# Input and forget gates of an mLSTM from the unnormalised input: split products on the normalised input against one full-precision product in four column groups

## The reference, cut to what matters

```python
def rms_norm(x, g):
    xf = x.astype(jnp.float32)
    out = xf * lax.rsqrt(jnp.mean(xf * xf, axis=-1, keepdims=True) + EPS)
    return (out * g.astype(jnp.float32)).astype(x.dtype)
...
    xn = rms_norm(x, lp['norm1_g'])
    z = xn @ lp['w_in'] + lp['b_in']
    sizes = [D_LRU, D_ML, D_ML, D_ML, D_ML, ML_HEADS, ML_HEADS, D_MODEL]
    u, q, k, v, o, ipre, fpre, ga, gb = jnp.split(z, np.cumsum(sizes).tolist(), axis=-1)
```

## Time and profile before

| what | value |
|---|---|
| time, median of 3 runs | 1068.19 us (1068.11 to 1069.31) |
| the profiled execution's own time | 1067.82 us |
| its span in the profile | 1066.0 us |
| TensorE (PE) busy | 1054.0 us, 99% |
| VectorE (DVE) busy | 620.0 us, 58% |
| ScalarE (ACT) busy | 388.5 us, 36% |
| GpSimd (POOL) busy | 371.1 us, 35% |
| granted clock of TensorE, mean | 0.999 |

### The profile page before, as it was taken

One profiled execution on the slowest core, in us unless ns is written; L12 is line 12 of the kernel. 1 busy time (PEld: TensorE's weight loads), 2 busy tenths in 40 slices (PEclk: granted clock), 3 DMA queues, 4 the chain that ended last, 5 costly groups with the idle time before them and its releaser, 6 DMA issues.

```text
span 1066.0 us, 19415 instructions
## 1 busy us (share of the span) xinstructions
PE 1054.0 (99%) x7974; PEld 1029.3 (97%) x7974; DVE 620.0 (58%) x971; ACT 388.5 (36%) x562; POOL 371.1 (35%) x180
## 2 busy tenths in 40 slices
PE   7999999999999999999999999999999999999997
PEld 6999999999999999999999999999999999999997
DVE  6777457854533343442543339999940189999413
ACT  6566787313332333232422333222211122222332
POOL 4333344333222222222223344334443344334330
PEclk9999999999999999999999999999999999999999
DMA  7433322346385592863443232322323222233312
GB/s 198 164 102 92 103 75 78 85 104 163 85 231 154 129 263 62 195 197 90 149 163 88 81 99 86 93 80 80 102 71 103 62 80 80 81 93 99 98 44 89
DMA packets 215696, 119.67 MB, mean 112 GB/s; under 512 B 39195, under 2 KB 212235, under 8 KB 215358
## 3 DMA queue, kind: packets, MB, share of 16 engines
q1 hardware_dynamic: 215404, 118.42, 39.4%
q10 hardware_dynamic: 210, 0.07, 0.0%
HBM read 97.49 MB, written 18.76 MB: 109 GB/s over the span
## 4 chain that ended last, share of the span: by engine, by line
PE 98%; ACT 1%; DMA 0%; POOL 0%; DVE 0%; issue 0%; SPq 0%; DVEq 0%
PE ring L2063 48%; PE ring L2481 22%; PE bank L2481 17%; PE bank L2353 2%; PE bank L2340 1%; PE bank L2110 1%; PE bank L2321 1%; PE bank L2333 1%; PE bank L2395 1%; PE bank L2220 1%; PE bank L2383 1%; PE bank L2418 0%; DMA x_tok<-in_x_prompt 0%; POOL x_split L917 0%; ACT sq_tok L1000 0%; PE bank L2527 0%
## 5 line engine op out<-in xcount | busy, mean ns | idle before, releaser
L2063 PE MATMUL ring<-x_split,whi 128*128 128x256 f32 (+1 forms) x2016 | 359.2, 300 | 0.0
L905 POOL TENSOR_TENSOR wlo<-stage,whi 128x1024 fp32r<-128x1024 f32 x78 | 194.2, 2490 | 411.7 <-ACT whi L963 411.7
L2063 PEld LDWEIGHTS ring<-x_split,whi 128*128 128x128 f32 x2016 | 303.9, 189 | 8.1 <-issue 7.6
L2063 PE MATMUL ring<-x_split,wlo 128*128 128x256 f32 (+1 forms) x1008 | 217.4, 297 | 0.0
L2063 PEld LDWEIGHTS ring<-x_split,wlo 128*128 128x128 f32 x1008 | 169.9, 189 | 0.0
L963 ACT ACTIVATE whi<-stage 128x1024 fp32r<-128x1024 f32 x80 | 84.3, 1054 | 92.3 <-PE ring L2063 81.2
L948 POOL TENSOR_TENSOR wlo<-stage,whi 128x1024 fp32r<-128x1024 f32 x28 | 71.7, 2560 | 108.4 <-ACT whi L1316 108.4
L2481 PE MATMUL ring<-x_split,whi 128*128 128x256 f32 (+1 forms) x512 | 88.7, 295 | 0.0
L1432 DVE SCALAR_TENSOR_TENSOR conv<-up,cols,conv 128x592 f32<-128x592 f32 x88 | 75.5, 858 | 3.1
L2481 PEld LDWEIGHTS ring<-x_split,whi 128*128 128x128 f32 x512 | 77.0, 189 | 0.0
L1969 DVE TENSOR_SCALAR conv<-up,cols 128x592 f32<-128x592 f32 x44 | 74.0, 1683 | 3.1
(11 more groups left out here) (365 smaller groups left out, 2053.3 us busy)
## 6 DMA issues: line engine op xcount, KB each, us to landing
stage<-in_w_in SPq DMA_DIRECT2D x56, 512.0 KB, 4.0
stage<-in_w_up SPq DMA_DIRECT2D x44, 512.0 KB, 3.7
stage<-in_w_down SPq DMA_DIRECT2D x16, 704.0 KB, 4.5
stage<-in_w_branch_a SPq DMA_DIRECT2D x8, 512.0 KB, 3.7
c_sample<-in_state_mlstm_C SPq DMA_DIRECT2D x16, 256.0 KB, 6.2
out_s_mlstm_C<-c_sample SPq DMA_DIRECT2D x16, 256.0 KB, 2.4
stage<-in_w_branch_b SPq DMA_DIRECT2D x8, 512.0 KB, 3.9
stage<-in_w_out SPq DMA_DIRECT2D x8, 512.0 KB, 3.8
```

The lines of the kernel that those rows point to most:

```text
L905: pool.tensor_tensor(spaced(wlo[:, slot]), packed(stage[:, slot, 0:n]), spaced(whi[:, slot]).bitcast(F32), ALU.subtract).then_inc(w_lo, 1)
L2063: last = pe.matmul(of(z, t0 or -2, t1), w[:, kk * WS:kk * WS + P], x_, start=kk == 0 and m == 0, stop=kk == kn - 1 and m == 2)
```

## The change

The gates are made from `x_raw` instead of from the split normalised x. GpSimd multiplies the 8 gate columns by `norm1_g` into a float32 tile `gate_w` (128 x 8 x 32, the rest of which is zeros). After the first tile of u, 16 full-precision matmuls with 128x32 weights, 296 tokens each, write banks 2 and 3; block kk uses the column group kk % 4, so that four partial sums stand on partitions 32j to 32j+31. VectorE multiplies them by `rrow` into `gate_z`, after `conv(0)`. Two more matmuls with a 128x36 matrix of zeros and ones (`gate_sel`, made by GpSimd from the identity) add the four partial sums and bring the two gates to partitions 0 and 32; they stand ahead of g = 2. ScalarE evicts them after `main_hi(2)`, and `lru_gates(0)`, ahead of g = 3, waits for that. The first tile of u takes `bank2(0)`. The 48 `gate_step` matmuls, the high and the low part of the gate weights, and the gates' tile number (so all later tile numbers are one less) go away, and `first_step` takes their place between the transposing jobs.

```diff
-T_GATE = T_COLS2 + 2
-T_U = T_GATE + 1
+T_U = T_COLS2 + 2
...
+        gate_w = sb("gate_w", [P, KT, 32], o_p - 2 * SLOT - 64)
+        gate_sel = sb("gate_sel", [P, GATE_W], o_p - SLOT - 64)
+        gate_z = sb("gate_z", [P, T], o_b + 7 * TB)
...
@@ GpSimd
-            pool.wait_ge(w_hi, 1)
-            pool.tensor_tensor(gate_columns(glo), gate_in_w.rearrange("p k (g h) -> p k g h", h=HEADS),
-                               gate_columns(ghi).bitcast(F32), ALU.subtract).then_inc(w_lo, 1)
+            pool.wait_ge(gate_w_in, 16)
+            pool.wait_ge(tile_evicted, T_COLS + 1)
+            pool.tensor_tensor(gate_w[:, :, 0:2 * HEADS], gate_in_w,
+                               cols[:, C_N1:C_N1 + KT].rearrange("p (k o) -> p k o", o=1).to_broadcast([P, KT, 2 * HEADS]),
+                               ALU.mult).then_inc(w_lo, 1)
             for n in range(2, 8):
                 xn_low(n)
+            sel_ = gate_sel[:, :]
+            sel = bass.AP(sel_.tensor, sel_.offset, [sel_.ap[0], [32, 2], [1, HEADS]])
+            st.link(pool.tensor_tensor(sel, gate_rows_of(ident[:, :], 0), gate_rows_of(ident[:, :], 1), ALU.add))
+            st.link(pool.tensor_tensor(sel, sel, gate_rows_of(ident[:, :], 2), ALU.add))
+            pool.tensor_tensor(sel, sel, gate_rows_of(ident[:, :], 3), ALU.add).then_inc(gate_sel_ready, 1)
...
@@ ScalarE
-            act.activation(gate_columns(ghi), gate_in_w.rearrange("p k (g h) -> p k g h", h=HEADS), ACT.Copy
-                           ).then_inc(w_hi, 1)
...
-            st(act.activation(gs[:, 0, :], of_first(bank2(0))[0:HEADS], ACT.Identity, bias=gbias[:, 0:1]))
-            act.wait_ge(tile_evicted, t)
-            act.activation(gs[:, 1, :], of_first(bank2(0))[32:32 + HEADS], ACT.Copy).then_inc(tile_evicted, 1)
...
+            def gate_evict():
+
+                act.wait_ge(gate_rows_in, 48)
+                act.wait_ge(gate_summed, 1)
+                st(act.activation(by_halves(gs[:, 0, :]), bank[0:HEADS, 2:4, 0:T // 2], ACT.Identity, bias=gbias[:, 0:1]))
+                act.activation(by_halves(gs[:, 1, :]), bank[32:32 + HEADS, 2:4, 0:T // 2], ACT.Copy
+                               ).then_inc(gate_evicted, 1)
+
             for g in range(31):
                 if g:
                     lru_period(g)
                 main_hi(g)
+                if g == 2:
+                    gate_evict()
@@ VectorE
             lru_rates()
             conv(0)
+            dve.wait_ge(gate_psum, 1)
+            dve.wait_ge(rb_ready, 2)
+            tt(by_halves(gate_z[:, :]), bank[:, 2:4, 0:T // 2], by_halves(rrow[:, :]), ALU.mult).then_inc(gate_scaled, 1)
             conv(1)
@@ TensorE
+            def gate_products():
+
                 pe.wait_ge(w_lo, 1)
-                return part_step(bank2(0), GATE_W, GATE_W, ghi, glo, kk, part)
+                pe.wait_ge(raw_done, XN)
+                pe.wait_ge(rb_ready, 2)
+                for hf in range(2):
+                    for kk in range(KT):
+                        j = kk % 4
+                        last = pe.matmul(bank[32 * j:32 * j + 32, 2 + hf, 0:T // 2], gate_w[:, kk, :],
+                                         x_raw[:, kk, T // 2 * hf:T // 2 * hf + T // 2], start=kk < 4, stop=kk >= 4,
+                                         tile_position=(0, 32 * j), skip_group_check=True)
+                last.then_inc(gate_psum, 1)
+
+            def gate_sums():
+
+                pe.wait_ge(gate_sel_ready, 1)
+                pe.wait_ge(gate_scaled, 1)
+                for hf in range(2):
+                    last = pe.matmul(bank[0:GATE_W, 2 + hf, 0:T // 2], gate_sel[:, :],
+                                     gate_z[:, T // 2 * hf:T // 2 * hf + T // 2], start=True, stop=True)
+                last.then_inc(gate_summed, 1)
...
             keep_clock(10)
-            gate_step(0, 0)
             rms_rows(1)
-            late_turn(8)
-            late_turn(9)
-            gate_step(0, 1)
-            late_turn(10)
-            late_turn(11)
-            gate_step(0, 2)
-            gate_step(0, 3)
-            gate_step(0, 4)
-            late_turn(12)
-            gate_step(0, 5)
-            late_turn(13)
-            gate_step(0, 6)
-            gate_step(0, 7)
-            gate_step(1, 0)
-            late_turn(14)
+            for n in range(8, 12):
+                late_turn(n)
             first_step(0, 0)
             first_step(0, 1)
-            gate_step(1, 1)
+            late_turn(12)
+            first_step(0, 2)
+            first_step(0, 3)
+            late_turn(13)
+            first_step(0, 4)
+            first_step(0, 5)
+            late_turn(14)
+            first_step(0, 6)
+            first_step(0, 7)
             late_turn(15)
-            for kk in range(2, 8, 2):
-                first_step(0, kk)
-                first_step(0, kk + 1)
-                if kk < 6:
-                    gate_step(1, 1 + kk // 2)
...
-            for kk in (4, 5, 6):
-                gate_step(1, kk)
-            gate_step(1, 7).then_inc(tile_done, 1)
             for kk in range(7):
                 first_step(1, kk)
             first_step(1, 7).then_inc(tile_done, 1)
+            gate_products()
...
@@ lru_gates(0), ahead of g = 3
                     pe.wait_ge(tile_evicted, T_U + 1)
+                    pe.wait_ge(gate_evicted, 1)
...
             for g in range(1, 16):
                 if g in LRU_TURN:
                     lru_gates(LRU_TURN.index(g))
+                elif g == 2:
+                    gate_sums()
```

More of the change, by code:

```diff
@@ L388, in hybrid_layer, with by_halves, gate_rows_of @@
         gate_in_w = stage[:, 0, D + 296:D + 296 + 8 * KT].rearrange("p (k c) -> p k c", c=8)
-        ghi, glo = whi3[:, 0:KT * GATE_W], wlo3[:, 0:KT * GATE_W]
-        def gate_columns(ap):
-            return bass.AP(ap.tensor, ap.offset, [ap.ap[0], [GATE_W, KT], [32, 2], [1, HEADS]])
+        gate_w = sb("gate_w", [P, KT, 32], o_p - 2 * SLOT - 64)
+        gate_sel = sb("gate_sel", [P, GATE_W], o_p - SLOT - 64)
+        gate_z = sb("gate_z", [P, T], o_b + 7 * TB)
+        def by_halves(ap):
+            return ap.rearrange("p (h t) -> p h t", h=2)
+        def gate_rows_of(ap, j):
+            return bass.AP(ap.tensor, ap.offset + 32 * j, [ap.ap[0], [HEADS, 2], [1, HEADS]])
         def spaced(w):
@@ L512, in hybrid_layer @@
         rms_done, x_sq = sem("rms_done"), sem("x_sq")
+        gate_sel_ready, gate_psum, gate_scaled, gate_summed, gate_evicted = (
+            sem("gate_sel_ready"), sem("gate_psum"), sem("gate_scaled"), sem("gate_summed"), sem("gate_evicted"))
         lam_abs, lam_exp, gate_abs, gate_exp, gates_ready = (
@@ L880, in _ @@
             st(pool.memset(bass.AP(xh.tensor, xh.offset - 2, [xh.ap[0], [1, 2]]).bitcast(F32), 0.0))
-            st(pool.memset(ghi.bitcast(F32), 0.0))
-            st(pool.memset(glo.bitcast(F32), 0.0))
+            st(pool.memset(gate_w[:, :, :], 0.0))
+            st(pool.memset(gate_sel[:, :], 0.0))
             st.wait()
@@ L902, in lo @@
             def lo(b, slot, n):
-                pool.wait_ge(w_hi, b + 1)
+                pool.wait_ge(w_hi, b)
                 pool.tensor_tensor(spaced(wlo[:, slot]), packed(stage[:, slot, 0:n]), spaced(whi[:, slot]).bitcast(F32),
@@ L1051, in _ @@
                 raw_copy(n + 4)
-            act.wait_ge(gate_w_in, 16)
-            act.wait_ge(const_done, 2)
-            act.activation(gate_columns(ghi), gate_in_w.rearrange("p k (g h) -> p k g h", h=HEADS), ACT.Copy
-                           ).then_inc(w_hi, 1)
             square_tile(4)
@@ L1080, in _ @@
                 columns(T_COLS2 + n, *COL_GROUPS[n])
-            t = T_GATE
-            act.wait_ge(gate_rows_in, 48)
-            act.wait_ge(tile_done, t + 1)
-            st(act.activation(gs[:, 0, :], of_first(bank2(0))[0:HEADS], ACT.Identity, bias=gbias[:, 0:1]))
-            act.wait_ge(tile_evicted, t)
-            act.activation(gs[:, 1, :], of_first(bank2(0))[32:32 + HEADS], ACT.Copy).then_inc(tile_evicted, 1)
             act.wait_ge(lam_abs, 1)
@@ L1148, in evict_u @@
                 t = T_U + g
-                z = bank2(1)[:, SPLIT - BEGIN:] if g == 0 else wide[t % 2]
+                z = bank2(0)[:, SPLIT - BEGIN:] if g == 0 else wide[t % 2]
                 bias = cols[:, C_BIN + g:C_BIN + g + 1]
@@ L1485, in _ @@
                 xn_scaled(n)
-            dve.wait_ge(w_hi, 2)
+            dve.wait_ge(w_hi, 1)
             dve.wait_ge(w_lo, 1)
@@ L1607, in gates_abs @@
             def gates_abs():
-                dve.wait_ge(tile_evicted, T_GATE + 1)
+                dve.wait_ge(gate_evicted, 1)
                 st.link(ts(f_, f_, gbias[:, 1:2], None, ALU.add))
@@ L1889, in _ @@
             b = B_WB + 1
-            dve.wait_ge(w_hi, b + 1)
+            dve.wait_ge(w_hi, b)
             dve.wait_ge(w_lo, b)
@@ L2112, in part_step @@
                 return last
-            def gate_step(part, kk):
+            def gate_products():
                 pe.wait_ge(w_lo, 1)
```

(10 more changed lines are left out.)

## The result

The changed kernel takes 1074.41 us in the median of five runs (1072.82 to 1075.41), the kernel before 1068.19 (1068.11 to 1069.31, five runs). The ratio is 1.0057, 95% interval 1.0045 to 1.0068: 6.2 us slower. The forecast was 1073.0 in a range of 1070.9 to 1076.0. The profiled execution took 1074.41 us, its span 1072.6, that is 6.6 us more than before.

The account below looks back on a forecast made before the run. The prediction took TensorE, busy 99% of the span, as the bound; two new waits of +2.15 and +2.6 us sum to +4.8, giving a median of 1073.0 us against 1068.19, range 1070.9 to 1076.0.

Parts of the forecast that it names:

- The work of TensorE: Gate matmuls: 6.7 us removed, 3.15 added (products 2.15, adding matmuls 1.0), so TensorE gains 3.5 us of pure work.
- The beginning: Up to g = 1: row transposes start at 25.5 us, TensorE idles about 3 us, g = 1 ends at 39.6.
- The clock: Rival, chance 0.12: TensorE's clock falls in the new idle stretches, giving 1074.5 to 1076.5 us.
- the likeliest case: Both new waits bind as forecast, chance 0.62; with the bounds of its costs, 1072 to 1074.5 us.
- First new wait: Before g = 2: adding matmuls wait 2.1 us for VectorE's scaling behind `conv(0)`; g = 2 starts at 42.75, +2.15 us.
- my own signs of being wrong: Early ScalarE evictions, products over 3 us, no TensorE idling before g = 2, or a later idle stretch shrinking by the loss.
- Second new wait: Before `lru_gates(0)`: TensorE waits for ScalarE's split after g = 2 and both gate evictions, +2.6 us.
- GpSimd's hold: Rival, chance 0.10: GpSimd's weight 4 split delays the third accumulation of `conv(0)` about 2 us; 1075.0 us.
- Only one wait binds: Rival, chance 0.06: VectorE's chain is 2 us quicker, leaving the second wait; +2.7 in sum, 1070.9 us.
- Faster: Rival, chance 0.04: TensorE's work alone decides and 3.5 us are saved; 1064.7 us.

Follow-up runs that it names:

- the products alone early: Changed kernel with the 16 gate products moved right behind transposing job 15, ScalarE's order as in the change; 1077.34 us, ratio 1.0092 to the kernel before.
- all early: Changed kernel with products behind transposing job 15, scaling behind the last `xn_low`, adding matmuls ahead of g = 1, evictions behind `evict_u(0)`; 1066.96 us.
- the fillers: Changed kernel plus thirty 128x128 filler transposes in TensorE's idle stretch ahead of the parameter rows; 1074.78 us, ratio 1.0068 to the kernel before.
- the early evictions: Changed kernel with ScalarE evicting the gates before `main_hi(2)` instead of after it; 1071.34 us, ratio 1.0029 to the kernel before.

## Why the prediction was right, and where it was not

The sign and the time came out in range, 1.4 us above the forecast. Point by point, by its own steps:

- **The work of TensorE.** The 16 products: forecast 2.15 us, measured 2.13 to 2.20 in the versions' chains. The column groups overlap as at line 2383. The adding matmuls: 1.0 forecast, 1.12. Not in the sum: a tile behind either of them takes 6.83 us where 6.60 stood, and `lru_gates(0)` 2.31 instead of 2.07 behind its wait, 0.7 us in all. TensorE's weight loads sit idle 0.48 us ahead of the first of these tiles.
- **The beginning.** `xn_scaled` of job 15 ended at 25.38, forecast 25.3. The rows' DMA, the one thing that no row showed, landed later than I took: the transposes started at 26.41, not 25.5 (bounds 25.3 and 26.9). That landing varies: the last of the rows' DMAs was issued at 21.73 in this execution, at 20.80 in the one before the change, and at 19.36 with the products alone early, where TensorE found the rows there at 25.17.
- **The clock.** The step that failed, though the total came out. I had it as a rival at 0.12, with the argument that the stretches were short, and the likeliest case had nothing for it. The first stretch was enough, 3.8 us long: 1.40 us in the transposes and 1.12 in the steps, 2.5 us. The price was too low as well: I had 1.2 to 1.7 us for one fall, from 2.4 to 3.4 us of work at half speed; it was 5.2 us of work, from 26.41 until between 31 and 32. (By these prices my bounds for the rival were 1074.2 to 1076.4, not 1074.5 to 1076.5. And the slow clock at the start of the kernel I worked out from the distances of the filler transposes alone: the granted clock reads 1.00 there.) The Trainium skill's page "TensorE: Matmul & The Clock Gate", section "What's actually happening", has idleness throttle the clock and activity release it. The trace of the changed kernel shows both; the fall between 16 and 17 us with all early shows that here the clock can also fall behind a stretch that is only partly idle.
- **First new wait, +2.15 us.** VectorE's scaling was done at 42.47 (forecast 41.7), but the wait did not bind, since TensorE came at 43.10 instead of 39.6. That TensorE would not idle before g = 2 was one of my own signs of being wrong. Start of g = 2: 44.22 against 42.75. What I had put down to VectorE was made by the DMA (0.9), the clock (2.5) and the slower tile (0.2): 3.6 us that took the place of a wait of 2.1. With the clock held, the wait came back (1.0 us).
- **Second new wait, +2.6 us.** Measured 2.6, with the releaser forecast; removed by exchanging the order of two steps, it gives 3.1 us. That is somewhat more than its length; 0.24 of it is `lru_gates(0)`, which takes 2.07 us again, the rest I can't place.
- **The rivals.** GpSimd's hold did not catch `conv(0)` in the change (2.65 us); it did, as described, when TensorE was made earlier (4.61). The scaling itself, with one operand in PSUM, took 0.76 to 0.78 us in all versions. In the one with the products alone early it began after GpSimd's split (38.48 to 41.00) had ended, so no run here tests it against a hold. "Only one wait binds" is what the trace shows, but not for its reason (VectorE was not quicker), and not at its time of 1070.9.
- **Faster, 0.04.** In this form no. With the same parts in other places yes, by 1.2 us, where TensorE's pure work had promised 3.5. In its profile g = 1 starts 1.1 us earlier than before the change. The rest stays with the rows' transposes, which wait for VectorE's chain and the DMA.

So the forecast named the second wait and its size rightly, and the total was right partly by luck, by two errors that cancel: 2.1 us for a wait that was not there, against 3.6 us for things that were small or absent in my sum.

## What to carry to other kernels

Work that is moved between engines costs most at its hand-overs: for each new wait, find what stands ahead of the releasing instruction in its own queue, and put the releaser where that engine is idle. Here the same instructions cost 6.2 us or win about 1.2, by their places alone. When work is taken out of a stretch that another resource bounds, TensorE goes idle there, and what follows may run at the lower clock; fill the stretch with work that is needed anyway. Making one engine earlier can also lose: here it let GpSimd's split begin ahead of VectorE's third accumulation, and that version is 3 us slower than the change. And before a step of a few tenths between two profiles is put down to an edit, look whether the stretches ahead of it were equally long.

## What the runs showed of the hardware

- The granted clock fell in or behind idle stretches of TensorE: in the changed kernel between 24 and 25 us, with TensorE idle from 22.6 to 26.4; with the fillers between 52 and 53, in or at the end of the wait of 2.6 us that ended at 52.72; with the products alone early between 40 and 41, in the wait of 5.2 us that ended at 42.50; with the early evictions between 26 and 27, when TensorE was at work again after 3.0 us of idling. The wait of 2.6 us in the changed kernel (51.1 to 53.7) left it at 1.00. In the profiles of two versions it fell between 16 and 17 us with TensorE at work, behind a stretch in which it was partly idle; in the others the same stretch left it at 1.00.
- It came back in the changed kernel between 31 and 32 us, after work since 26.4; with the fillers between 56 and 57, after work since 52.7.
- The five runs of the change have mean granted clocks of 0.993 to 0.997 and lie 2.6 us apart; the last 33 of the kernel before have 0.998 to 1.000 and lie 2.0 us apart. A mean clock of 0.996 or less stands beside the slowest runs of most versions.
- Fillers of 128x128 transposes kept the granted clock at 1.00 over the stretch from 22 to 26 us.
- A tile behind the 16 products (128x32 weights) or the two adding matmuls (128x36) took about 0.2 us longer than one behind another tile. Behind `lru_gates(0)`, also in full precision but with 128x128 weights, nothing of the kind shows (three tiles in 19.76 us, 6.59 each). What in the narrow matmuls costs it, no run here tests.
- While GpSimd split a weight (35.38 to 37.76 in the changed kernel), a VectorE instruction of 8 columns took 2.39 us instead of 0.17.
